# An encoder layer on Trainium2: a new order for the first HGRN head, and three output tiles added by DMAs from GpSimd

## The reference

```python
h = rms_norm(x, g_pre_mix)
z = h @ w_in                                   # 1024 -> 10240 columns
q_a, k_a, v_a, g_a, q_b, f_b, i_b, g_b, m_a, m_b = split(z)
o_a = retention(rope(q_a), rope(k_a) / 16, v_a)               # 4 heads of 256
y_a = (silu(g_a) * head_rms(o_a)) @ w_a
f = lb + (1 - lb) * sigmoid(f_b)
o_b = hgrn2(q_b, 1 - f, i_b, log(f))           # 8 heads of 128: S_t = diag(f_t) S_{t-1} + k_t v_t^T, o_t = S_t^T q_t
y_b = (silu(g_b) * head_rms(o_b)) @ w_b
x = x + rms_norm((sigmoid(m_a) * y_a + sigmoid(m_b) * y_b) @ w_out, g_post_mix)
u = square(relu(rms_norm(x, g_pre_ffn) @ w_up))               # 4096 columns
y = x + rms_norm(u @ w_down, g_post_ffn)
```

## Time and profile before

| | |
|---|---|
| Time, median of 3 runs | 2416.68 us (2416.2 to 2418.96) |
| The profiled execution | 2416.9 us, its span 2414.4 us, so 2.5 us lie around the span |
| TensorE clock granted over the span | 0.999 of full speed |
| PE (matmul) busy | 2390.8 us (99%), 13,984 instructions |
| DVE busy | 1280.2 us (53%) |
| ACT busy | 750.0 us (31%) |
| POOL busy | 487.9 us (20%) |
| DVE low part of a weight block, L1363 | 128 times, 1249 ns in the mean |
| Queries of head 0 (second of the three loads of L493) | issued at 650.8 us, landed 8.2 us later |
| DMA queues in use | SP's (255.89 MB) and two for instructions; none of POOL |

### The profile page before, as it was taken

How to read it: one execution, slowest core, us unless ns; L and a number is a source line. 1 busy time by engine, 2 the same in 40 slices (tenths; PEclk the granted TensorE clock), 3 DMA queues, 4 the chain that set the end, 5 groups by cost and what they waited for, 6 DMA issues and landing times.

```text
span 2414.4 us, 36796 instructions
## 1 busy us (share of the span) xinstructions
PE 2390.8 (99%) x13984; PEld 2267.8 (94%) x13984; DVE 1280.2 (53%) x2404; ACT 750.0 (31%) x1454; POOL 487.9 (20%) x730
## 2 busy tenths in 40 slices
PE   8999999999999999999999999999999999999999
PEld 8999999999989999999999999889899899898896
DVE  4153525243376667667765444544655645646638
ACT  4133332323222222232222332324233233332334
POOL 1021202111165456536544000001000000000001
PEclk9999999999999999999999999999999999999999
DMA  5252725354424323432432634223102101101104
GB/s 176 93 193 68 244 71 189 125 180 128 137 87 139 124 85 114 142 107 95 139 131 84 225 115 152 98 88 97 53 18 70 44 25 64 49 26 61 41 24 161
DMA packets 219213, 257.25 MB, mean 107 GB/s; under 512 B 8164, under 2 KB 186728, under 8 KB 218984
## 3 DMA queue, kind: packets, MB, share of 16 engines
q1 hardware_dynamic: 219112, 255.89, 31.8%
HBM read 175.64 MB, written 80.22 MB: 106 GB/s over the span
## 4 chain that ended last, share of the span: by engine, by line
PE 75%; issue 11%; DVE 7%; POOL 3%; DMA 2%; ACT 1%; SPq 1%; POOLq 0%; DVEq 0%; ACTq 0%
PE bank L627 11%; PE bank L628 11%; PE bank L629 11%; PE bank L902 6%; PE bank L903 6%; PE bank L904 6%; PE bank L951 5%; PE bank L952 5%; PE bank L950 5%; PE bank L818 1%; PE bank L931 1%; PE bank L930 1%; PE bank L932 1%; DMA ZQ<-scratch_z 1%; POOL ORS L1862 1%
## 5 line engine op out<-in xcount | busy, mean ns | idle before, releaser
L627 PE MATMUL bank<-XH,WHI 128*128 128x384 f32 x2256 | 769.9, 341 | 0.9 <-issue 0.6
L629 PE MATMUL bank<-XH,WLO 128*128 128x384 f32 x2256 | 755.1, 335 | 0.0
L628 PE MATMUL bank<-XL,WHI 128*128 128x384 f32 x2256 | 754.8, 335 | 0.0
L627 PEld LDWEIGHTS bank<-XH,WHI 128*128 128x128 f32 x2256 | 424.2, 188 | 5.4 <-issue 3.2
L628 PEld LDWEIGHTS bank<-XL,WHI 128*128 128x128 f32 x2256 | 424.3, 188 | 0.8
L629 PEld LDWEIGHTS bank<-XH,WLO 128*128 128x128 f32 x2256 | 423.8, 188 | 0.0
L1363 DVE TENSOR_TENSOR WLO<-WRAW,WHI 128x1024 fp32r<-128x1024 f32 x128 | 159.9, 1249 | 241.9 <-ACT WHI L1021 237.6
L1021 ACT ACTIVATE ZST<-bank 128x384 f32<-128x384 f32 x240 | 117.3, 490 | 526.6 <-PE bank L629 517.6
L902 PE MATMUL bank<-XH,WHI 128*128 128x384 f32 x768 | 256.8, 334 | 1.6 <-ACT XH L1021 1.6
L904 PE MATMUL bank<-XH,WLO 128*128 128x384 f32 x768 | 256.7, 334 | 0.0
L903 PE MATMUL bank<-XL,WHI 128*128 128x384 f32 x768 | 256.6, 334 | 0.0
(11 more groups left out here) (221 smaller groups left out, 3487.6 us busy)
## 6 DMA issues: line engine op xcount, KB each, us to landing
scratch_z<-ZST SPq DMA_DIRECT2D x80, 576.0 KB, 3.1
WRAW<-in_w_in SPq DMA_DIRECT2D x80, 512.0 KB, 3.9
HZ<-scratch_z SPq DMA_DIRECT2D x32, 576.0 KB, 5.2
WRAW<-in_w_up SPq DMA_DIRECT2D x32, 512.0 KB, 4.2
WDR<-in_w_down SPq DMA_DIRECT2D x32, 512.0 KB, 5.4
MG<-scratch_z SPq DMA_DIRECT2D x16, 576.0 KB, 5.5
ZQ<-scratch_z SPq DMA_DIRECT2D x4, 1152.0 KB, 6.6
ZK<-scratch_z SPq DMA_DIRECT2D x4, 1152.0 KB, 8.7
```

The lines of the kernel that those rows point to most:

```text
L627: pe.matmul(psum[c][:, 0:CH], WHI[p][:, k, :], XH[:, k, s], start=(k == 0), stop=False)
L628: pe.matmul(psum[c][:, 0:CH], WHI[p][:, k, :], XL[:, k, s], start=False, stop=False)
L629: last = pe.matmul(psum[c][:, 0:CH], WLO[p][:, k, :], XH[:, k, s], start=False, stop=(k == KT - 1))
```

## The change

- **First head.** ACT's `forget(0)` becomes two sigmoids, of columns 0 to 383 and of the other 768. DVE makes f and k of the first 384 columns, waits for the queries, runs `prep_q(0, 0, 0)`, `wlo_block(41, 1)`, `prep_q(0, 0, 1)`, and then f and k of the other 768. `H.fk` and `H.f_ok` are counted one higher from there on. POOL sets the first 384 columns of RR to one ahead of its wait, and waits for the second `H.fk` after `prep_k(0, 0)`. PE's wait for `H.fk` goes.
- **All eight heads.** On DVE `wlo_block` stands behind `weights` in its slot (slots 3, 6, 9, 12). On POOL the power of tile 0 (`head_rs(H, h, 0)`) moves from behind the two gates into `prep_k(h, 1)`, behind level 5.
- **The end.** PE takes positions 2, 4 and 6, DVE adds at 5, 7 and 8, and for positions 0, 1 and 3 (tiles 4, 5 and 7) SP stores x1 straight to the output in the middle of the program; at the end DVE only scales these tiles in place, and POOL issues a DMA each that adds the 512 KB to the output in HBM (`accum_op`). Only six tiles of x1 are loaded again, each output tile has its own buffer, and POOL issues its DMAs between the powers.

```diff
-        Y_PE = (2, 4, 6, 7)
-        Y_DVE = (0, 1, 3, 5, 8)
+        Y_PE = (2, 4, 6)
+        Y_DMA = (0, 1, 3)
+        Y_DVE = (5, 7, 8)
+        Y_OUT = (2, 4, 5, 6, 7, 8)
+        T_DMA = [Y_ORDER[j] for j in Y_DMA]
...
+            def x1_store(t):
+
+                dst = y_rows(t) if t in T_DMA else x1s[t * P:(t + 1) * P, :]
+                sp.dma_start(dst, X1R[t % 2][:, :]).then_inc(x1_st[t % 2], 16)
...
                 if t == 0:
                     pe.wait_ge(H.in_[2], 16 * h + 16)
-                    pe.wait_ge(H.fk, h + 1)
...
+            def forget_first():
+                act.wait_ge(H.in_[1], 16)
+                act.activation(FG[:, 0:CH], HZ[1][:, 0:CH], ACT.Sigmoid).then_inc(H.f_ok, 1)
+                act.activation(FG[:, CH:], HZ[1][:, CH:], ACT.Sigmoid).then_inc(H.f_ok, 1)
...
-                        if c == 0 and jj:
-                            wlo_block(n + 1, (jj + 1) % 2)
                         if s in (1, 6, 7):
                             if s == 6:
                                 dve.wait_ge(H.sc, 9 * h + 3)
                             prep_q(h, 1 + s // 6, 0 if s < 7 else 1)
                         if s >= HA and s - HA < NT:
                             weights(h, s - HA)
+                        if c == 0 and jj:
+                            wlo_block(n + 1, (jj + 1) % 2)
...
+            def forget_first(s, ready):
+
+                dve.wait_ge(H.f_ok, ready)
+                ch(dve.tensor_scalar(FG[:, s], FG[:, s], LBC[:, 1, 0:1], LBC[:, 0, 0:1], ALU.mult, ALU.add))
+                ch(dve.tensor_scalar(KK[:, s], FG[:, s], -1.0, 1.0, ALU.mult, ALU.add))
+                dve.sem_inc(H.fk, 1)
+
             ret_done(dve)
+            forget_first(slice(0, CH), 1)
+            dve.wait_ge(H.in_[0], 16)
+            prep_q(0, 0, 0)
             wlo_block(41, 1)
-            forget(0)
-            prep_q(0, 0, 0)
             prep_q(0, 0, 1)
+            forget_first(slice(CH, T), 2)
...
                 if j in Y_PE:
+                    scaled.then_inc(y_tt, 1)
+                elif j in Y_DMA:
+                    scaled.then_inc(y_sc, 1)
+                else:
+                    ch(scaled)
+                    dve.wait_ge(x_in[j], 32)
+                    dve.tensor_tensor(dst, dst, X1F[j][:, :], ALU.add).then_inc(y_ok, 1)
...
-                prep_k(h, 1)
+                prep_k(h, 1, {5: 0})
                 for c in range(2):
                     gate(H, h, c, 1, HZ[3][:, c * CH:(c + 1) * CH].unsqueeze(1))
-                head_rs(H, h, 0)
                 head_rs(H, h, 1)
...
+            ch(pool.memset(RR[:, 0:CH], 1.0))
             pool.wait_ge(H.fk, 1)
-            prep_k(0, 0)
+            prep_k(0, 0, fresh=False)
+            pool.wait_ge(H.fk, 2)
...
+            def y_onto(i):
+
+                t = Y_ORDER[Y_DMA[i]]
+                pool.wait_ge(y_sc, i + 1)
+                pool.dma_start(y_rows(t), ACC[:, t, :], accum_op=ALU.add).then_inc(y_ac, 16)
+
+            y_power(0)
+            y_power(1)
+            y_onto(0)
+            y_power(2)
+            y_power(3)
+            y_onto(1)
+            y_power(4)
+            y_power(5)
+            y_onto(2)
+            for j in range(6, NT):
+                y_power(j)
```

More of the change, by code:

```diff
@@ L266, in program @@
         y_tt, y_pe, y_pk = sem("y_tt"), sem("y_pe"), sem("y_pk")
-        y_st = [sem(f"y_st{i}") for i in range(NOF)]
+        y_st, y_ac, y_sc = sem("y_st"), sem("y_ac"), sem("y_sc")
         zs, us, x1s = scr["z"], scr["u"], scr["x1"]
@@ L338, in program, with y_rows, y_buf @@
         Y_ORDER = (4, 5, 6, 7, 0, 1, 2, 3, 8)
-        Y_PE = (2, 4, 6, 7)
-        Y_DVE = (0, 1, 3, 5, 8)
+        Y_PE = (2, 4, 6)
[3 more added lines that the diff above has]
+        T_DMA = [Y_ORDER[j] for j in Y_DMA]
+        def y_rows(t):
+            return o["y_p"][0, t * P:(t + 1) * P, :] if t < NTP else o["y_s"].rearrange("b t d -> (b t) d")
+        def y_buf(j):
+            return OF[Y_OUT.index(j)]
         def y_store(sp, j):
-            t = Y_ORDER[j]
             if j in Y_PE:
@@ L347, in y_store @@
                 sp.wait_ge(y_ok, Y_DVE.index(j) + 1)
-            dst = o["y_p"][0, t * P:(t + 1) * P, :] if t < NTP else o["y_s"].rearrange("b t d -> (b t) d")
-            sp.dma_start(dst, OF[j % NOF][:, :]).then_inc(y_st[j % NOF], 16)
+            sp.dma_start(y_rows(Y_ORDER[j]), y_buf(j)[:, :]).then_inc(y_st, 16)
         def ret_mixed(e):
@@ L565, in _ @@
                     sp.wait_ge(d_x1, t)
-                    sp.dma_start(x1s[(t - 1) * P:t * P, :], X1R[(t - 1) % 2][:, :]).then_inc(x1_st[(t - 1) % 2], 16)
+                    x1_store(t - 1)
             sp.wait_ge(d_x1, NT)
-            sp.dma_start(x1s[(NT - 1) * P:, :], X1R[(NT - 1) % 2][:, :]).then_inc(x1_st[(NT - 1) % 2], 16)
+            x1_store(NT - 1)
             def up_w(g, b):
@@ L590, in _ @@
             sp.dma_start(GF[:, :], a["g_post_ffn"].to_broadcast([P, D])).then_inc(gb_in, 16)
-            for j in range(NT):
+            for j in Y_OUT:
                 t = Y_ORDER[j]
                 sp.dma_start(X1F[j][:, :], x1s[t * P:(t + 1) * P, :]).then_inc(x_in[j], 16)
-            for j in range(NT):
+            for j in Y_OUT:
                 y_store(sp, j)
-            for i in range(NOF):
-                sp.wait_ge(y_st[i], 16 * ((NT + NOF - 1 - i) // NOF))
+            sp.wait_ge(y_st, 16 * len(Y_OUT))
+            sp.wait_ge(y_ac, 16 * len(Y_DMA))
             sp.wait_ge(H.sr_st, 16 * HH + 16)
@@ L1007, in _ @@
             y_x1(0)
-            for i in range(4):
-                if i < 3:
+            for i in range(len(Y_PE)):
+                if i < len(Y_PE) - 1:
                     y_x1(i + 1)
@@ L1216, in hg_pair @@
                         piece(2 * KT + x)
-            forget(0)
+            forget_first()
             with act.Fori(0, HH // 2 - 1) as i:
@@ L1345, in _ @@
             for i, j in enumerate(Y_PE):
-                if j >= NOF:
-                    act.wait_ge(y_st[j % NOF], 16 * (j // NOF))
                 for q in range(2):
                     act.wait_ge(y_pe, 2 * i + q + 1)
-                    last = copy(OF[j % NOF][:, 512 * q:512 * (q + 1)], psum[2 * i + q][:, :])
+                    last = copy(y_buf(j)[:, 512 * q:512 * (q + 1)], psum[2 * i + q][:, :])
                 last.then_inc(y_pk, 1)
@@ L1574, in forget @@
             def forget(h):
-                dve.wait_ge(H.f_ok, h + 1)
+                dve.wait_ge(H.f_ok, h + 2)
                 ch(dve.tensor_scalar(FG[:, :], FG[:, :], LBC[:, 1, bass.ds(h, 1)], LBC[:, 0, bass.ds(h, 1)],
@@ L1727, in finish @@
                 dve.wait_ge(y_rs, j + 1)
+                dve.wait_ge(gb_in, 32)
+                dst = y_buf(j)[:, :] if j in Y_DVE else ACC[:, t, :]
+                scaled = dve.scalar_tensor_tensor(dst, ACC[:, t, :], yrs[:, t:t + 1], GF[:, :], ALU.mult, ALU.mult)
                 if j in Y_PE:
[L1729 to L1738, removed]
+                    scaled.then_inc(y_tt, 1)
[5 more added lines that the diff above has]
+                    dve.tensor_tensor(dst, dst, X1F[j][:, :], ALU.add).then_inc(y_ok, 1)
             def up_lo(g, b):
@@ L1907, in _, with prep_k @@
             ch.reset()
-            def prep_k(h, c, after={}):
+            def prep_k(h, c, after={}, fresh=True):
                 s = slice(c * CH, (c + 1) * CH)
@@ L1913, in prep_k @@
                 pool.tensor_tensor(FT[:, 0:CH // 2], FG[:, c * CH:(c + 1) * CH:2], FG[:, c * CH + 1:(c + 1) * CH:2], ALU.mult)
-                ch(pool.memset(RR[:, s], 1.0))
+                if fresh:
+                    ch(pool.memset(RR[:, s], 1.0))
                 for l in range(LEV):
@@ L1957, in hg_head @@
                 if not last:
-                    pool.wait_ge(H.fk, h + 2)
+                    pool.wait_ge(H.fk, h + 3)
                     pool.wait_ge(H.att, 9 * h + 10)
@@ L1981, in _, with y_power @@
             pool.memset(ACC[:, :, :], 0.0).then_inc(acc0, 1)
-            for j in range(NT):
+            def y_power(j):
                 t = Y_ORDER[j]
```

## The result

The changed kernel takes 2420.64 us in the median of 22 runs, the kernel before 2417.41 us beside it: the ratio is 1.0015, with a 95% interval of 1.0009 to 1.0020. The change costs 3.2 us. The interval lies above 1, so the loss is real, but it is less than the 0.2% that was to count as a difference. The profiled execution took 2420.39 us, its span 2418.5 us.

The account below looks back on a forecast made before the run. PE was busy 99% of the span, so only its waits and the two ends could give time; -3.9 + 8.3 - 2.3 = +2.1 us on 2416.9 gave 2419.0, as a median 2418.8, range over the cases 2409.5 to 2424.

Parts of the forecast that it names:

- -3.9 + 8.3 - 2.3: Forecast terms in us: first head gains 3.9, moved power costs heads 1 to 7 8.3, the end gains 2.3.
- First tile of head 0: PE's first hg_a in head 0 would start at 671.64 without its wait for keys, gaining 3.2 us.
- Second tile: Before head 0's second hg_a, PE would newly wait 1.8 us for DVE's weights, leaving 1.4 us of the gain.
- The low clock: PE's half-speed clock at 691 to 692 in head 0, said to follow two idle stretches and to go.
- the first stall: PE's 3.2 us wait for POOL's keys before the first hg_a of head 0, forecast to go.
- The second stall: PE's 2.2 us wait for head 0's scaled output tile; with its low clock, 4.0 us gained by the moved power.
- The 1.5 us that I took off head 0 for late weights: In head 0, PE would find the fourth tile's weights late, losing 1.5 us.
- The price in heads 1 to 7: Moved power beside prep_q costs DVE 1.4 us a head, less 1.5 for the last two heads' room: 8.3 us.
- My rival: POOL locks DVE out in heads 1 to 7, costing the whole 2.2 us a head: 2424.4 us, chance 0.13.
- The end: At the tail, ACT's last copy comes earlier, so the last store starts sooner: 2.4 us gained, 2.3 taken.
- the fifth gap: Sign: PE's gap before the fifth hg_a of heads 1 to 5 grows by some 1.4 us.
- wait L809 for ATT grown to 10 us: Sign: PE's total wait for DVE's attention weights grows from 0.4 to about 10 us; under 3 us refutes the forecast.

Follow-up runs that it names:

- e3: The change's new end alone, on the kernel before: 2415.09 us, ratio 0.9992.
- e4: The low part behind the attention weights alone, on the kernel before: 2415.11 us, ratio 0.9992.
- e2: The changed kernel with the power of tile 0 back behind the two gates: 2409.70 us, ratio to before 0.9969.
- e5: The changed kernel with the power of tile 0 behind all of prep_k(h, 1), ahead of the gates: 2410.18 us, ratio to before 0.9973.
- e6: The new order of the first head alone, on the kernel before: 2415.18 us, ratio 0.9994.
- e1: The moved power of tile 0 alone (inside prep_k(h, 1), behind level 5), on the kernel before: 2428.17 us, ratio 1.0049.
- e8: The changed kernel with the power of tile 0 behind level 4 of prep_k(h, 1) instead of level 5: 2414.61 us, ratio to before 0.9994.
- e11: e9 with the gates waiting as in e10 and, in the first head, the power of tile 0 behind level 4: 2405.99 us, ratio to before 0.9956.
- e10: The changed kernel with one more wait, so POOL's two gates start only after prep_q(h, 1, 1): 2410.42 us, ratio to before 0.9971.
- e9: e5 with weights(0, 0) ahead of prep_q(0, 1, 0) in the first head: 2409.99 us, ratio to before 0.9973.
- e7: The changed kernel with the power of tile 0 behind level 6 of prep_k(h, 1) instead of level 5: 2415.95 us, ratio to before 0.9998.

## Why the prediction was right, and where it was not

**The total** was forecast at 2418.8, measured at 2420.6: no difference of over 0.2%, the likeliest case. Of the sum, -3.9 + 8.3 - 2.3, the profile has -2.2 + 7.8 - 1.5 = +4.1, which is the difference of the spans; the median moved by 3.2. Both gains were put too high. The 2.2 of the first head come about as follows.

**First tile of head 0.** 671.83 against 671.6. The keys of chunk 0 end at 671.43 against 670.7, still ahead of PE.

**Second tile.** The new wait was forecast at 1.8 us and is 2.35. `prep_q(0, 1, 0)` took 4.85 us, not 4.2: of the two rows between which I chose, the one beside the start of a `prep_k` was nearest, and I took less. The terms of my sum give 678.6, and I put down 679.2; it was 680.12.

**The low clock** was the step that failed. I wrote that it came behind two idle stretches, not behind the first alone, and so costed the new wait at its bare length. It came behind this single wait, and behind the first stall in e3 and e4: 1.6 us in the gap behind it, unforeseen. From one execution I had read an order that the next did not keep.

**The second stall** left with its low clock, the 4.0 us forecast (10.50 us before the fourth `hg_a` became 6.51). But I had put this down to the moved power, and that is not what did it here: in e2, e5 and e6 the power isn't moved into `prep_k`, and the gap is 6.51 to 6.54 all the same. The power alone, on the old order, removes the stall too (e1). Either is enough, and I had charged heads 1 to 7 with the dearer one. The 1.5 us that I took off head 0 for late weights came to 0.7 (gaps of 7.06 and 6.65).

**The price in heads 1 to 7** came out right in size, 7.8 against 8.3. The growth of `prep_q` was forecast well, since I took it from a stretch of the trace that had the same collision (6.08 us; the heads then showed 6.11). The sum has some luck in it: by e2 the moved power costs 9.2 us there, and the low part, which I had put at nothing, gives 1.5 back. Nor had the last two heads the room for which I took off 1.5: heads 6 and 7 lost 1.2 us each, heads 1 to 5 together 5.3. The reason that I gave was half right. I ascribed it to the amount of overlap, and e8 shows that a larger amount costs less. The Trainium skill (SBUF — State Buffer, Who interferes with whom) says that a VectorE instruction with two SBUF inputs excludes a GpSimd one that reads SBUF, and that one with at most one SBUF input, outside the 2-port perf modes, doesn't contend. The traces agree with both halves, one instruction at a time: a product takes 1.15 us beside one of 1.00 us, and `weights` with an operand in PSUM keeps its 1.10 beside a gate. The condition may matter here: VectorE's copy of 128x384 from SBUF to SBUF, with one input, takes 0.35 us alone and 1.04 where it starts beside GpSimd's first product of `prep_k(0, 1)` (672.82 in the kernel after); no run shows in which mode it ran. My rival took this rule for the whole 2.2 us and would have been wrong; as a rule on which pairs collide it gave the remedy, which I had not seen in it.

**The low part behind the weights** I had given nothing. It is worth some 1.5 us in heads 1 to 7 (e4), and it is part of why the 7.8 fits.

**The end.** 1.45 us against 2.3. POOL's three issues take 0.88 to 1.03 us, less than the 3 us that would have delayed the powers, and their landing of 5.6 us is hidden, as forecast.

**What would show it.** Of the signs that I named, the fifth gap (1.06 us longer in head 1, 1.4 forecast) and `prep_q` near 6.1 us held. The sign "wait L809 for ATT grown to 10 us" did not: it is 3.5 us. I had called the forecast wrong under 3 us, and it stays above only by the 2.35 us of head 0; heads 1 to 7 have 1.2 us of it, while the loss is there. So the sign was a bad one. Part of the loss is booked on the output tile one operation earlier, and much in no row of this view.

## What to carry to other kernels

When work on GpSimd is moved, look at what VectorE is running at its new time: products and copies out of SBUF that start beside a long GpSimd product end only behind it, operations that read PSUM keep their length. A wait that parks GpSimd until VectorE reaches its PSUM work is one line; here it took back the 10 us that the moved power had cost, as leaving the power where it was would have done. Before an operation is moved to cure a stall, try whether the rest of the change cures it. And a wait in the middle of an engine's list holds back all behind it: put the dependent operation where its input is just ready, not as early as the order allows.

## What the runs showed of the hardware

- A VectorE product of 128x192 takes 0.35 us alone and 1.15 to 1.18 us when it starts just behind a GpSimd product of 128x384 (1.00 us). Where GpSimd products of 0.5 to 0.75 us stretch it, it takes 0.54 to 0.85. In the second head after, the ones that start at 772.53 and 773.99 end 0.21 us behind the GpSimd instruction that was running (772.47 to 773.47, 773.72 to 774.93). The one that comes second is stretched, on either engine: in e8 the VectorE product that began 0.01 us ahead of the gates kept its 0.56 us, and the gates took 2.40, where they take 1.98 to 2.00 with only the weights beside them (e11, e10).
- The VectorE side of this holds with one exception: in the thirteen traces 2,192 products of `prep_q` start while a GpSimd product of 192 or 384 columns is running, and 2,191 end behind it. Of 1,193 operations of `weights` with an operand in PSUM that start so, 847 end while it is still running, and all keep their length within 0.01 us.
- A VectorE copy of 128x384 from SBUF to SBUF takes 0.35 us alone and 1.04 to 1.07 where it starts together with the first product of a `prep_k` (672.82 and 743.52 in the kernel after).
- In the first head the granted clock fell to 0.50 behind the first idle stretch of PE over 2 us in ten kernels: of 2.1 us (e9), 2.3 to 2.4 (after, e7, e8, e10), 2.8 (e2, e5), 3.2 (e3), 3.3 (e4) and 3.7 (e6). It stayed at 1.00 behind one of 3.2 us in two (before, e1). Each fall costs PE some 1.6 to 1.9 us over a slot, beside the wait itself.
- The issue of a DMA from GpSimd that adds 512 KB onto HBM takes 0.88 to 1.03 us, and it lands in 5.6 us; SyncE's last store of as much takes 0.43 us before and 0.33 after to issue, and its stores of the output land in 2.6 to 3.9 (medians).
